# A two-block transformer layer on one core: 512-column products in the gate-and-up stage `gu2`, norms summed by halves after `out2` and `wo2`, and the bias rows copied before the second weight slab

## The chip, the core and the metric

The kernel runs on one core of a Trainium2 chip, as one launch. The metric is the device time of that launch in microseconds, the median of several runs. A profiled execution gives, beside its own time, one record per instruction: start, duration and what released it. Matrix products run on TensorE (PE), elementwise work on VectorE (DVE) and ScalarE (ACT); GpSimd (POOL) and SyncE (SP) here issue DMAs.

## The reference, cut to what matters

The whole computation is one hybrid layer (three attentions, a gated merge, a convolved feed-forward) and then a second block on the same 256 tokens of width 1024. The change touches mostly the second block, and a small table of the first:

```python
def second_block(x, mem, ...):
    mem_n = rms_norm(mem, mem_norm_g)
    h = rms_norm(x, g[0])                      # in2: convolution and RWKV mixing
    ...
    y = jnp.concatenate([y_conv, y_rwkv], axis=-1) @ w_out[i]      # stage out2
    x = x + rms_norm(y, g[1])                                      # norm y1
    y = memory_cross_attention(rms_norm(x, g[2]), mem_n, wq[i], wkv[i], wo[i])   # g2, wq, wo2
    x = x + rms_norm(y, g[3])                                      # norm y3
    y = swiglu(rms_norm(x, g[4]), w_gu[i], w_down[i])              # g4, gu2, down2
    x = x + rms_norm(y, g[5])                                      # norm y5
```

`rms_norm(y, g)` divides each row by the root of its mean square (plus 1e-6) and multiplies by a gain. `swiglu` multiplies by `w_gu` (1024 x 5632), takes silu of the first half times the second, and multiplies by `w_down` (2816 x 1024). In the first block the relative-position bias is a table of 12 heads spread over distances and added to attention scores.

## The kernel before, in words

All products are in fp32 precision made of three: each operand is split into a high part, rounded to the fast type, and the rest, and high x high, high x low and low x high are summed in PSUM (function `three`). The weights come as 126 slabs of 128 x 2048 floats (1 MB). For each slab SP starts the DMA into one of four buffers `raw` when the slab that lay there is used (`slab_used`), ACT makes `w_hi` (`split`, L481), DVE makes `w_lo` (`split`, L1003), and PE waits for `lo_ready`. ACT and DVE run one slab ahead. Each engine has one program in order, written out by hand, and semaphores tie them.

**Feature stages** (`up`, `gu2`, `wq` and others, function `features`) have the weights stationary, 128 columns at a time, and the 256 tokens moving: for each slab two column tiles `c`, in each eight depths `k`, in each three products of 256 columns, 48 in all. A slab's result is a "unit"; unit `u` lies in PSUM bank `u % 2` and must be taken out (`out_freed`) before PE starts unit `u + 2`. **Token stages** (`out2`, `wo2`, `down2`, function `token_products`) have the tokens stationary and 512 weight columns moving; token tile 0 ends in banks 4 and 5, tile 1 in 6 and 7, each bank with half of the 1024 columns. The first two slabs of `up` and `gu2` are computed token-wise by `first_pair`/`token_half`, tile 0 before tile 1, so that PE can start while tile 1 is still being normed.

**`gu2`** has 22 slabs in 11 pairs: even units are gates, odd units values. For pair `p`, ACT takes silu of the gate from PSUM (L958), DVE multiplies it with the value from PSUM (L1691), ACT copies the product's high part to `gT_hi` (L971), DVE subtracts for `gT_lo` (L1285). Pair 0 comes out turned and is transposed by PE into bank 6 (`turn_gu2`) in the middle of slab 3.

**A norm of a product** (`y1` after `out2`, `y3` after `wo2`) runs so for each token tile: ACT squares all 1024 columns from PSUM with a running sum (L498), then takes the root (L503); DVE multiplies PSUM by the gain (L1619), inverts the root (L1033), and scales and adds to `x` (L1625). Then comes the next norm of `x` itself: ACT squares `x` and takes the root, DVE writes `xn` (L1050), PE transposes it (L1780), ACT and DVE split the transposed tile into `hT_hi` (L521) and `hT_lo` (L1057). The last norm, `y5` tile 1, is already done by halves of 512 columns in `before`: PE finishes the first half of the columns first, ACT squares it while PE does the second half, DVE turns that sum into a bias for the root.

**The bias rows**: at the start PE spreads the bias table into PSUM (L1947, L1948), ACT copies the rows out (L563, L564) after its split of slab 2, POOL writes them to DRAM (L426) and reads them back as a sliding 1.5 MB plus 0.75 MB pattern (L432), and DVE adds them to the scores of group 0 (L1129).

## Time and profile before

| | |
|---|---|
| median of three runs | 871.76 us |
| lowest and highest | 871.37 and 872.42 us |
| profiled execution, its own time | 872.74 us |
| its span, first to last instruction | 870.9 us |
| PE busy | 852.4 us (98%) |
| DVE busy | 566.8 us (65%) |
| ACT busy | 445.0 us (51%) |
| granted TensorE clock | 0.998 |

A busy time adds up instructions, a span runs from the first to the last. Matmuls overlap by a modelled tail, so what one product costs in a stream is the distance from its start to the next one's, not its own duration. "Idle before" is the time in which an engine had nothing running before an instruction, with what released it.

### The profile page before, as it was taken

What the parts mean: (1) busy time and instruction counts of PE and PEld (TensorE: products, weight loads), DVE (VectorE), ACT (ScalarE), POOL (GpSimd) and SP (SyncE); (2) the same over time, 40 slices, a digit from 0 to 9 for tenths busy, and PEclk for the clock granted to TensorE, in tenths of its full rate; (3) what the DMA queues carried; (4) which work ended last, traced back from release to release, by engine and by line L of the source; (5) the groups of instructions that cost most, each with busy time, mean ns of one, the idle gap of its engine ahead of it and who ended that gap; (6) DMA issues with size and microseconds to landing.
All of it is one profiled execution on the core that took longest, in us unless ns stands there. A gap on an engine that the chain in (4) does not pass through costs nothing.

```text
span 870.9 us, 18537 instructions
## 1 busy us (share of the span) xinstructions
PE 852.4 (98%) x7972; PEld 790.7 (91%) x7972; DVE 566.8 (65%) x674; ACT 445.0 (51%) x571; POOL 20.8 (2%) x31
## 2 busy tenths in 40 slices
PE   8999999999999999999999999999999999999997
PEld 6989999989999998889997899988987999999885
DVE  6486565575977877638799974667554655545443
ACT  6546855454855566536574311546555544443432
POOL 1110000000000002000000000000000000000000
PEclk9999999999999999999999999999999999999999
DMA  8644454565655555455641211245424455555551
GB/s 333 245 166 146 152 178 154 181 217 199 236 168 182 188 193 186 158 187 177 217 169 71 99 50 53 99 148 194 167 97 150 167 191 193 170 175 186 193 193 49
DMA packets 22114, 145.40 MB, mean 167 GB/s; under 512 B 2603, under 2 KB 2795, under 8 KB 5922
## 3 DMA queue, kind: packets, MB, share of 16 engines
q1 hardware_dynamic: 19008, 134.23, 44.2%
q0 software_dynamic: 2896, 10.13, 3.4%
q8 instruction: 54, 0.88, 0.4%
q14 instruction: 10, 0.08, 0.0%
q10 hardware_dynamic: 146, 0.07, 0.0%
HBM read 143.35 MB, written 1.07 MB: 166 GB/s over the span
## 4 chain that ended last, share of the span: by engine, by line
PE 78%; DVE 10%; DMA 5%; ACT 4%; issue 2%; SPq 0%; POOL 0%; DVEq 0%; ACTq 0%
PE ps L1739 22%; PE ps L1741 21%; PE ps L1740 21%; DMA raw<-in_weights 3%; PE ps L1865 3%; DVE cacc L1383 3%; PE ps L2231 2%; DVE w_lo L1003 2%; DMA bias<-bias_scratch 2%; ACT w_hi L481 1%; PE ps L2426 1%; PE ps L2442 1%; PE ps L2014 1%; PE ps L1805 1%; ACT sc L591 1%
## 5 line engine op out<-in xcount | busy, mean ns | idle before, releaser
L1003 DVE TENSOR_TENSOR w_lo<-raw,w_hi 128x2048 fp32r<-128x2048 f32 x125 | 287.3, 2302 | 126.7 <-ACT w_hi L481 126.5
L1739 PE MATMUL ps<-hT_hi,w_hi 128*128 128x256 f32 x1128 | 321.8, 285 | 0.9 <-ACT sig L636 0.5
L1740 PE MATMUL ps<-hT_lo,w_hi 128*128 128x256 f32 x1128 | 319.1, 283 | 0.0
L1741 PE MATMUL ps<-hT_hi,w_lo 128*128 128x256 f32 x1128 | 319.1, 283 | 0.0
L481 ACT ACTIVATE w_hi<-raw 128x2048 fp32r<-128x2048 f32 x125 | 238.8, 1913 | 138.3 <-DMA raw<-in_weights 138.3
L1739 PEld LDWEIGHTS ps<-hT_hi,w_hi 128*128 128x128 f32 x1128 | 216.3, 192 | 5.5 <-issue 3.6
L1740 PEld LDWEIGHTS ps<-hT_lo,w_hi 128*128 128x128 f32 x1128 | 216.4, 192 | 0.1
L1741 PEld LDWEIGHTS ps<-hT_hi,w_lo 128*128 128x128 f32 x1128 | 216.4, 192 | 0.0
L1741 PE MATMUL ps<-w_hi,gT_lo 128*128 128x512 f32 x176 | 69.3, 394 | 0.0
L1740 PE MATMUL ps<-w_lo,gT_hi 128*128 128x512 f32 x176 | 68.8, 391 | 0.0
L1739 PE MATMUL ps<-w_hi,gT_hi 128*128 128x512 f32 x176 | 68.7, 390 | 0.0
L1302 DVE SCALAR_TENSOR_TENSOR ub<-ps,pvec,ub 128x255 f32<-128x255 f32 (+1 forms) x88 | 38.4, 477 | 25.1 <-ACT ub L676 22.0
L1739 PE MATMUL ps<-w_hi,hT_hi 128*128 128x512 f32 (+2 forms) x128 | 47.0, 368 | 0.0
L1740 PE MATMUL ps<-w_lo,hT_hi 128*128 128x512 f32 (+2 forms) x128 | 46.3, 362 | 0.0
L1741 PE MATMUL ps<-w_hi,hT_lo 128*128 128x512 f32 (+2 forms) x128 | 46.3, 362 | 0.0
L676 ACT ACTIVATE ub<-ps,pvec 128x256 f32<-128x256 f32 x44 | 22.4, 561 | 44.7 <-PE ps L1741 44.7
L1740 PEld LDWEIGHTS ps<-w_lo,gT_hi 128*128 128x128 f32 x176 | 33.0, 188 | 7.5
L1739 PEld LDWEIGHTS ps<-w_hi,gT_hi 128*128 128x128 f32 x176 | 33.1, 188 | 7.1
L1741 PEld LDWEIGHTS ps<-w_hi,gT_lo 128*128 128x128 f32 x176 | 33.1, 188 | 6.9
L1285 DVE TENSOR_TENSOR gT_lo<-ub,gT_hi 128x512 f32 (+1 forms) x21 | 14.5, 688 | 32.4 <-ACT gT_hi L971 31.7
L958 ACT ACTIVATE ub<-ps 128x512 f32<-128x512 f32 x11 | 6.6, 597 | 43.2 <-PE ps L1741 43.1
L1739 PEld LDWEIGHTS ps<-w_hi,hT_hi 128*128 128x128 f32 x128 | 24.1, 189 | 4.5 <-issue 0.7
(325 smaller groups left out, 1187.6 us busy)
## 6 DMA issues: line engine op xcount, KB each, us to landing
raw<-in_weights SPq DMA_DIRECT2D x126, 1024.0 KB, 4.9
row_gain<-in_rows_vec POOLq DMA_DIRECT2D x4, 512.0 KB, 3.9
norm_gain<-in_rows_vec POOLq DMA_DIRECT2D x4, 512.0 KB, 5.5
bias<-bias_scratch POOLq DMA_DIRECT2D x1, 1536.0 KB, 12.7
x<-in_x SPq DMA_DIRECT2D x2, 512.0 KB, 3.9
xn<-in_mem POOLq DMA_DIRECT2D x2, 512.0 KB, 5.9
out<-x SPq DMA_DIRECT2D x4, 256.0 KB, 2.1
masks<-in_masks POOLq DMA_DIRECT2D x1, 768.0 KB, 11.0
```

The costliest lines, as they stand in the source:

```text
L481: A(w_hi[:, n % RAW, :], raw[:, n % RAW, :], ACT.Copy).then_inc(sems["hi_ready"], 1)
L591: A(sc[:, g % 2, i, s:e], sc[:, g % 2, i, s:e], ACT.Exp, bias=ast[:, 88 + col:89 + col], accum_out=ast[:, 120 + col:121 + col]).then_inc(s ...
L676: A(ub[:, p % 2, s, c, :], src[:, c * T:(c + 1) * T], ACT.Identity, bias=pvec[:, bass.ds(p + 2 * turn, 1), col + 3], scale=pvec[:, bass.ds ...
L1003: V.tensor_tensor(w_lo[:, n % RAW, :], raw[:, n % RAW, :], w_hi[:, n % RAW, :].bitcast(F32), ALU.subtract).then_inc(sems["lo_ready"], 1)
L1285: V.tensor_tensor(gT_lo[:, bass.ds(2 * p + 4 * turn, 2), :], src, gT_hi[:, bass.ds(2 * p + 4 * turn, 2), :].bitcast(F32), ALU.subtract)\
L1302: ins = V.scalar_tensor_tensor(out=dst, in0=src[:, c * T:(c + 1) * T - lag], scalar=pvec[:, bass.ds(p + 2 * turn, 1), 4 * (2 * s + c) + ta ...
L1383: ins = V.scalar_tensor_tensor(out=dst, in0=src, scalar=vec[:, col:col + 1], in1=dst, op0=ALU.mult, op1=ALU.add)
L1739: mm(dst, left[0], right[0], start=first, stop=False)
L1740: mm(dst, left[0], right[1], start=False, stop=False)
L1741: return mm(dst, left[1], right[0], start=False, stop=last)
L1865: last = mm(dst, part[:, k, cols], right[:, k * T:(k + 1) * T], start=(part is hT_hi and k == 0 and right is hi), stop=(part is hT_lo and ...
L2231: last = mm(ps[to, b + q, j * CHUNK:(j + 1) * CHUNK], left[rows, 8 * q + j, :], right(rows, 8 * q + j), start=True, stop=True)
```

## The change

**1. `gu2` with 512-column products.** `hT_hi` and `hT_lo` become the two halves of one tile `hT`. From slab 2 of `gu2` on, the new function `doubled` replaces `features`: for each column tile and depth it multiplies the high weights by high and low tokens side by side (512 moving columns, one bank) and adds the low weights times the high tokens on the second half (256 columns). A unit now takes two banks, 0 and 1 or 2 and 3, and its two halves must be added: DVE does it with a `tensor_reduce` over the pair (`gu_sum`), for the gate and for the value. ACT takes silu in place in SBUF, DVE multiplies in SBUF. `doubled` waits for bank 1 before its second column tile in the first doubled slab, as unit 81 (value of pair 0) lies there.

**2. Half-column sums.** `sumsq_halves` (ACT) and `add_halves` (DVE) are the code of `y5` tile 1 as functions, now used for both tiles of `y1` and `y3` also; the product stages before them (`out2`, `wo2`) finish the last slab by halves for both token tiles. After `y1`, the norm `g2` is written in two halves per tile, and ACT fills `hT_hi` before its next split and before the last memory unit is taken out.

**3. The head of `gu2`.** DVE's subtraction for slab 1 is cut in two: one half before the norm of tile 0, the other behind it, with a signal `lo_rest` for the second. `first_pair` runs high rows of both slabs, then low rows of both, and transposes tile 1 only after these.

**4. Bias rows.** ACT copies them before its split of slab 2.

```diff
@@ ACT, the start
-            splits(2)
             act.wait_ge(sems["bias_ps_ready"], 1)
             A(bias_row[0:4, 0, :], ps[0:4, 6, 0:BIAS_ROW], ACT.Copy).then_inc(sems["bias_row_ready"], 1)
             A(bias_row[0:8, 1, :], ps[0:8, 7, 0:BIAS_ROW], ACT.Copy).then_inc(sems["bias_row_ready"], 1)
+            splits(2)
@@ ACT, norms and gu2
+            def sumsq_halves(name, stage, t, halves_ready):
+
+                act.wait_ge(sems["acc_half"], halves_ready)
+                A(tok[:, 0, 0, :], bank(4 + 2 * t), ACT.Square, accum_out=stat[:, 40:41]).then_inc(sems["half_sum"], 1)
+                acc_tile(stage)(t)
+                col = 4 * STATS[name] + t
+                A(tok[:, 0, 1, :], bank(5 + 2 * t), ACT.Square, accum_out=stat[:, col:col + 1]).then_inc(sems["sumsq_ready"], 1)
+                act.wait_ge(sems["half_bias"], halves_ready)
+                act.wait_ge(sems["sumsq_ready"], STAT_AT[name, t])
+                A(stat[:, col + TT:col + TT + 1], stat[:, col:col + 1], ACT.Sqrt, scale=1.0 / D, bias=stat[:, 41:42])\
+                    .then_inc(sems["rms_ready"], 1)
...
-            sumsq("y1", lambda t: banks(4 + 2 * t, 2), acc_tile("out2"))
+            for t in range(TT):
+                sumsq_halves("y1", "out2", t, 1 + t)
...
             sumsq("g2", lambda t: x[:, t, :], x_tile("y1"))
+            fill_normed("g2")
             splits(FIRST_SLAB["wq"])
             memory_out(7)
-            fill_normed("g2")
...
-            sumsq_acc("y3", "wo2", 0)
+            sumsq_halves("y3", "wo2", 0, 3)
             splits(FIRST_SLAB["gu2"])
             sumsq_tile("g4", "y3", 0)
-            sumsq_acc("y3", "wo2", 1)
+            sumsq_halves("y3", "wo2", 1, 4)
             fill_tile("g4", 0)
...
+                if p == 0:
+                    A(gate, unit(u, turn), ACT.Silu).then_inc(out_freed[u % 2], 1)
+                else:
                     gu_high(p - 1, turn)
+                    if p >= 2:
+                        act.wait_ge(sems["g_lo_ready"], PAIRS + p - 1 + 2 * turn)
+                    act.wait_ge(out_freed[u % 2], u // 2 + 1 + 2 * turn)
+                    A(gate, gate, ACT.Silu).then_inc(sems["gate_silu"], 1)
                 split(n + 2 + AHEAD, turn)
@@ DVE, norms
+            def half_bias(halves_ready):
+
+                dve.wait_ge(sems["half_sum"], halves_ready)
+                V.tensor_scalar(stat[:, 41:42], stat[:, 40:41], 1.0 / D, EPS, ALU.mult, ALU.add).then_inc(sems["half_bias"], 1)
...
-            add_normed("y1", 1)
-            normed("g2")
+            for t in range(TT):
+                add_halves("y1", 1, t, 1 + t, 1)
+            normed("g2", (0,), 2)
+            normed("g2", (1,), 2)
...
-            add_normed("y3", 2, tiles=(0,))
-            splits(FIRST_SLAB["gu2"])
+
+            add_halves("y3", 2, 0, 3, 1)
+            n = next_slab[0]
+            next_slab[0] += 1
+            dve.wait_ge(sems["hi_ready"], n + 1)
+            V.tensor_tensor(w_lo[:, n % RAW, 0:SLAB // 2], raw[:, n % RAW, 0:SLAB // 2],
+                            w_hi[:, n % RAW, 0:SLAB // 2].bitcast(F32), ALU.subtract).then_inc(sems["lo_ready"], 1)
             normed("g4", (0,), 2)
-            add_normed("y3", 2, lambda: fill_tile("g4", 0), tiles=(1,))
+            V.tensor_tensor(w_lo[:, n % RAW, SLAB // 2:], raw[:, n % RAW, SLAB // 2:],
+                            w_hi[:, n % RAW, SLAB // 2:].bitcast(F32), ALU.subtract).then_inc(sems["lo_rest"], 1)
+            add_halves("y3", 2, 1, 4, 1)
+            fill_tile("g4", 0)
             normed("g4", (1,), 2)
             fill_tile("g4", 1)
@@ DVE, gu2
+            def gu_sum(p, s, u, turn):
+
+                dve.wait_ge(sems["slab_used"], UNIT_SIGNAL[u][1] + 4 * turn)
+                both = ps[:, 2 * (u % 2):2 * (u % 2) + 2, :]
+                evacuated(u, V.tensor_reduce(ub[:, p % 2, s, :, :], both.rearrange("p c (h n) -> p c n h", h=2), AX.X, ALU.add))
...
+                    gu_sum(p, 0, u, turn)
                 split(n + 2 + AHEAD, turn)
...
+                    dve.wait_ge(sems["gate_silu"], p + 2 * turn)
+                    gu_sum(p, 1, u + 1, turn)
+                    wait_unit(u + 1, turn)
+                    V.tensor_tensor(value, gate, value, ALU.mult).then_inc(sems["gated_value"], 1)
@@ PE
+            def doubled(n, u, turn=0, between=None):
+
+                bank_free(u, turn)
+                hi, lo = slab(n, turn)
+                for c in range(2):
+                    if c and between:
+                        between()
+                    if c and u == FIRST_UNIT["gu2"] + 2:
+                        pe.wait_ge(out_freed[(u - 1) % 2], (u - 1) // 2 + 1)
+                    dst = bank(2 * (u % 2) + c)
+                    for k in range(KD):
+                        w = slice(k * T + c * P, k * T + (c + 1) * P)
+                        mm(dst, hi[:, w], hT[:, :, k, :], start=(k == 0), stop=False)
+                        last = mm(dst[:, T:2 * T], lo[:, w], hT_hi[:, k, :], start=False, stop=(k == KD - 1))
+                return last
...
+                if stage == "gu2":
+                    for low_rows in (False, True):
+                        for s in range(2):
+                            token_half(stage, name, s, 0, low_rows)
+                    transposes(name, 1)
```

PE, one depth after another in slab 2 of `gu2`, before (`w_hi` and `w_lo` are the weight parts, `hT_hi` and `hT_lo` the token parts):

```order
L1739 MATMUL ps<-hT_hi,w_hi 128x256
L1740 MATMUL ps<-hT_lo,w_hi 128x256
L1741 MATMUL ps<-hT_hi,w_lo 128x256
L1739 MATMUL ps<-hT_hi,w_hi 128x256
L1740 MATMUL ps<-hT_lo,w_hi 128x256
L1741 MATMUL ps<-hT_hi,w_lo 128x256
```

and the same place now:

```order
L1805 MATMUL ps<-hT,w_hi 128x512
L1806 MATMUL ps<-hT,w_lo 128x256
L1805 MATMUL ps<-hT,w_hi 128x512
L1806 MATMUL ps<-hT,w_lo 128x256
```

Three products of 256 columns became one of 512 and one of 256; the columns streamed are the same 768.

DVE between the end of `wo2` and the second pair of `gu2`, before (`xn`, `x` the normed and the running tokens, `ub` the gate and value buffers):

```order
L1619 TENSOR_TENSOR xn<-ps,row_gain 128x1024
L1033 RECIPROCAL stat<-stat 128x1
L1625 SCALAR_TENSOR_TENSOR x<-xn,stat,x 128x1024
L1003 TENSOR_TENSOR w_lo<-raw,w_hi 128x2048
L1033 RECIPROCAL stat<-stat 128x1
L1050 SCALAR_TENSOR_TENSOR xn<-x,stat,norm_gain 128x512 x2
L1619 TENSOR_TENSOR xn<-ps,row_gain 128x1024
L1057 TENSOR_TENSOR hT_lo<-ps,hT_hi 128x4x128 x2
```

and now:

```order
L1634 TENSOR_SCALAR stat<-stat 128x1
L1644 TENSOR_TENSOR xn<-ps,row_gain 128x512 x2
L1036 RECIPROCAL stat<-stat 128x1
L1648 SCALAR_TENSOR_TENSOR x<-xn,stat,x 128x1024
L1706 TENSOR_TENSOR w_lo<-raw,w_hi 128x1024
L1036 RECIPROCAL stat<-stat 128x1
L1053 SCALAR_TENSOR_TENSOR xn<-x,stat,norm_gain 128x512 x2
L1709 TENSOR_TENSOR w_lo<-raw,w_hi 128x1024
L1634 TENSOR_SCALAR stat<-stat 128x1
L1644 TENSOR_TENSOR xn<-ps,row_gain 128x512 x2
```

The second `TENSOR_SCALAR` (the bias for the root of tile 1) stands behind the second half of the split, and `hT_lo` of tile 0 has moved behind the whole of tile 1's norm.

DVE in `gu2`, second pair, before:

```order
L1003 TENSOR_TENSOR w_lo<-raw,w_hi 128x2048
L1285 TENSOR_TENSOR gT_lo<-ps,gT_hi 128x512
L1003 TENSOR_TENSOR w_lo<-raw,w_hi 128x2048
L1691 TENSOR_TENSOR ub<-ub,ps 128x512
```

and now:

```order
L1006 TENSOR_TENSOR w_lo<-raw,w_hi 128x2048
L1288 TENSOR_TENSOR gT_lo<-ps,gT_hi 128x512
L1720 TENSOR_REDUCE ub<-ps 128x512
L1006 TENSOR_TENSOR w_lo<-raw,w_hi 128x2048
L1720 TENSOR_REDUCE ub<-ps 128x512
L1738 TENSOR_TENSOR ub<-ub 128x512
```

Two reductions per pair are new; the gate's stands between the low part of the product before and the second split.

## Rows read from the trace of the kernel before

**Rows 1.** The page's first part: busy time and share by engine.

```profile
PE 852.4 (98%) x7972; PEld 790.7 (91%) x7972; DVE 566.8 (65%) x674; ACT 445.0 (51%) x571; POOL 20.8 (2%) x31
```

**Rows 2.** The waits of PE: who, for whom, us in total, times, longest.

```profile
PE ps L1780 <- DVE xn L1050: 3.5, 4, 1.6
PE ps L2001 <- DVE ast L1187: 1.2, 1, 1.2
PE ps L1805 <- ACT hT_hi L521: 1.2, 1, 1.2
```

**Rows 3.** Timeline (start us, duration, engine, line), ACT: silu of two gates in succession.

```profile
718.80 0.60 ACT L958 ACTIVATE ub<-ps 128x512 f32<-128x512 f32 x1 [4.73 <-PE ps L1741]
...
730.31 0.60 ACT L958 ACTIVATE ub<-ps 128x512 f32<-128x512 f32 x1 [4.54 <-PE ps L1741]
```

**Rows 4.** Timeline, PE: 512-column streams in `out2` (first two) and `down2` (last two).

```profile
597.29 0.39 PE L1741 MATMUL ps<-w_hi,hT_lo 128*128 128x512 f32 x1
...
602.05 0.39 PE L1741 MATMUL ps<-w_hi,hT_lo 128*128 128x512 f32 x1
...
856.41 0.39 PE L1739 MATMUL ps<-w_hi,gT_hi 128*128 128x512 f32 x1
...
864.65 0.39 PE L1739 MATMUL ps<-w_hi,gT_hi 128*128 128x512 f32 x1
```

**Rows 5.** Timeline, DVE: a reduction over 1024 elements, and a scan over 256.

```profile
43.25 1.21 DVE L1139 TENSOR_REDUCE ast<-sc 128x4 f32<-128x1024 f32 x1
...
45.03 0.68 DVE L1181 TENSOR_TENSOR_SCAN sig<-masks,sig 4x256 f32<-4x256 f32 x1
```

**Rows 6.** The page's fifth part: costliest groups (busy, mean ns | idle before, releaser).

```profile
L1003 DVE TENSOR_TENSOR w_lo<-raw,w_hi 128x2048 fp32r<-128x2048 f32 x125 | 287.3, 2302 | 126.7 <-ACT w_hi L481 126.5
...
L481 ACT ACTIVATE w_hi<-raw 128x2048 fp32r<-128x2048 f32 x125 | 238.8, 1913 | 138.3 <-DMA raw<-in_weights 138.3
...
L1285 DVE TENSOR_TENSOR gT_lo<-ub,gT_hi 128x512 f32 (+1 forms) x21 | 14.5, 688 | 32.4 <-ACT gT_hi L971 31.7
```

**Rows 7.** Timeline, y3 tile 0 (whole) and y5 tile 1 (second half): square, then add.

```profile
667.59 1.03 ACT L498 ACTIVATE tok<-ps 128x1024 f32<-128x1024 f32 x1 [3.30 <-PE ps L1741]
...
670.14 1.29 DVE L1625 SCALAR_TENSOR_TENSOR x<-xn,stat,x 128x1024 f32<-128x1024 f32 x1
...
865.54 0.60 ACT L987 ACTIVATE tok<-ps 128x512 f32<-128x512 f32 x1 [0.69 <-PE ps L1741]
...
867.06 1.41 DVE L1713 SCALAR_TENSOR_TENSOR x<-xn,stat,x 128x512 f32<-128x512 f32 x2
```

**Rows 8.** Timeline, head of `gu2`: transposes on PE, fills on ACT, the value product on DVE.

```profile
674.54 1.32 PE L1780 MATMUL ps<-masks,xn 128*128 128x128 f32 x8 [1.55 <-DVE xn L1050]
...
681.42 1.32 PE L1780 MATMUL ps<-masks,xn 128*128 128x128 f32 x8 [0.35 <-DVE xn L1050]
...
675.30 1.26 ACT L521 ACTIVATE hT_hi<-ps 128x512 fp32r<-128x512 f32 x2 [0.82 <-PE ps L1780]
...
682.17 1.26 ACT L521 ACTIVATE hT_hi<-ps 128x512 fp32r<-128x512 f32 x2 [1.79 <-PE ps L1780]
...
691.24 0.68 DVE L1691 TENSOR_TENSOR ub<-ub,ps 128x512 f32<-128x512 f32 x1
```

**Rows 9.** Timeline, DVE between `out2` and `wq`: the low fills.

```profile
610.62 2.49 DVE L1057 TENSOR_TENSOR hT_lo<-ps,hT_hi 128x512 fp32r<-128x512 f32 x4 [1.30 <-ACT hT_hi L521]
```

**Rows 10.** Timeline, the start: bias copies, slab splits and exponentials on ACT, bias sum on DVE, DMA on SP.

```profile
21.35 0.46 ACT L563 ACTIVATE sig<-ps 4x384 f32<-4x384 f32 x1
...
30.40 1.91 ACT L481 ACTIVATE w_hi<-raw 128x2048 fp32r<-128x2048 f32 x1
...
39.60 1.91 ACT L481 ACTIVATE w_hi<-raw 128x2048 fp32r<-128x2048 f32 x1 [1.86 <-DMA raw<-in_weights]
...
44.70 0.40 ACT L591 ACTIVATE sc<-sc,ast 128x128 f32<-128x128 f32 x1 [1.41 <-DVE ast L1150]
...
40.79 1.82 DVE L1129 TENSOR_TENSOR sc<-ps,bias 128x768 f32<-128x768 f32 x2 [5.13 <-DMA bias<-bias_scratch]
...
30.04 0.33 SPq L390 DMA_DIRECT2D raw<-in_weights  x1
```

More of the change, by code:

```diff
@@ L1820, in first_slab, with token_products @@
                 first_features(FIRST_SLAB[stage], FIRST_UNIT[stage], ready)
-            def token_products(name, left, ready, then=None, together=1, halves=False):
+            def token_products(name, left, ready, then=None, together=1, halves=()):
                 n0, count = FIRST_SLAB[name], dict(STAGE_SLABS)[name]
@@ L1828, in product @@
                     hi, lo = slab(n0 + i)
-                    by_half = halves and t == 1 and i == count - 1
+                    by_half = t in halves and i == count - 1
                     for one, other in itertools.product(range(2), range(2)):
```

118 lines of the change are left out of this document (60 added, 58 removed).

## The prediction

> **What bounds the kernel now.** I read the page's busy times first, then PE's waits, then the timelines where the change acts. PE is busy 852.4 us of 870.9 [rows 1], so only two things can shorten the kernel much: a cheaper stream of products, or the 18.5 us in which PE has none. Of those the waits name the ones that this change can reach: four waits for `xn`, 3.5 us, of which 1.55 and 0.35 stand at the head of `gu2`; 1.2 us for the first fill of `wq`; 1.2 us for DVE in the first attention group [rows 2, 8]. DVE and ACT have room on average (65% and 51%) [rows 1], but DVE gets new work in `gu2`, so its order there must be followed too.
>
> **1. Products of 512 columns.** Two silus lie 11.51 us apart with 96 products between them, so a 256-column product costs 119.9 ns in a stream [rows 3]. In `out2`, 21 products of 512 columns take 4.76 us, 226.7 ns each; in `down2`, 36 take 8.24 us, 228.9 ns [rows 4]. The difference 226.7 - 119.9 = 106.8 ns is what 256 more columns cost at 2.4 GHz, so about 13.2 ns is fixed per product. Per depth: before 3 x 119.9 = 359.7 ns, after 226.7 + 119.9 = 346.6 ns, 13.1 ns less. A slab has 16 depths: 0.21 us less, 5.55 instead of 5.76 us. For 20 slabs 4.2 us; by the `down2` interval 10.9 ns a depth, 3.5 us. Not shown is a moving operand that lies in two pieces, as `hT[:, :, k, :]` does. From below it costs nothing, as the pieces are 256 floats each; from above I take the whole fixed part a second time, 13.2 ns, which eats the gain. I take nothing: within a piece the reads are those of every row here.
>
> Here a rule of the Trainium skill speaks against the size. TensorE: Matmul & The Clock Gate, section "Back-to-back issue gap", gives a warm interval of N/2.4 + 2.5 ns; by its fixed part 320 fewer products would save 0.8 us, not 4.2. The trace disagrees at 13.2 ns, though it can't say whether that part goes with the product or with the kind of stream.
>
> **2. Does DVE keep up?** Per pair DVE gets two reductions over 1024 PSUM elements. A reduction over 1024 elements takes 1.21 us from SBUF [rows 5]; I take 1.2. Per element the slowest DVE row is the scan, 0.68 us for 256 [rows 5]; at that rate one would take 2.7 us, the upper end. The loop that must fit into a pair, 2 x 5.55 = 11.1 us, runs from one gate sum to the next: ACT silu until its next start 0.5, ACT split 1.94, DVE split 2.21, value sum 1.2, multiplication 0.6, DVE split 2.21, low part 0.6, gate sum 1.2 [rows 5, 6] (on one engine the next start comes about 0.1 us before the end that a duration says). That is 10.5 us, with register work some 10.7: it fits, with 0.4 us to spare. So from slab 3 on `gu2` stays with PE: 19 x 0.21 = **4.0 us** saved. What hides 2.4 us of new DVE work per pair is DVE's idleness before; the wait for the gate sum on ACT has a 1.9 us split queued behind it, which is in the loop above.
>
> **3. Between `wo2` and slab 3 of `gu2`.** For y3 tile 0 the add starts 2.55 us after the square of 1024 columns; in the halved form of y5, 1.52 us after the second square [rows 7]. So the add of tile 0 starts at 669.1 instead of 670.14. Then only half a split (1.2 us) stands before the norm instead of 2.3 [rows 6], and `xn` is there at 672.9; PE ends `wo2` at 674.54 - 1.55 = 673.0, so this wait [rows 8] goes. But a new wait appears. ACT must take the root of y3 tile 1 before it fills `hT_hi` of tile 0, and that root waits for the half bias, which DVE gives only after both halves of `xn` (673.5) and the second half of the split (674.7). The fill starts at 675.0, against 675.30 [rows 8]. Of 1.55 us only 0.3 to 0.4 us is left.
>
> After that PE has 48 products before the transposes of tile 1 instead of 40, so these start at 681.4 as before (681.42), and `xn` is there. Their fill starts at 682.1, against 682.17 [rows 8]. Low rows no longer stand between transposes and high rows, so PE starts tile 1 at 682.7 and slab 2 at 688.5, 0.8 us sooner than before. Now what is late next: the second column tile of slab 2 needs bank 1, free when DVE has multiplied the value of pair 0. It did so 691.24 + 0.68 - 682.17 = 9.75 us after the fill [rows 8], through ACT's split, table load, silu, split and DVE's split, which the change leaves alone: 691.85. PE would want it at 688.5 + 8 x 0.347 = 691.3, and waits 0.6 us. Slab 3 starts at 694.65 instead of 695.05: **0.4 us** gained, slab 2's 0.21 included. If nothing stalled it would be 1.0; if the half bias is later by a fill, 0.
>
> In slab 3 the turned pair passes ACT 0.6, DVE 0.6 and the gate sum 1.2: bank 0 is free 2.45 us after the transposes, PE needs it after 2.77. Value sum 1 ends about 0.05 us late for slab 5. I count 0.
>
> **4. y1 to `wq`.** PE is covered by the last memory slab while the norm runs, so the earlier root buys little; DVE is serial here, and gets two more half instructions per norm, some 0.6 us until the last `xn`. But ACT fills at once instead of after a split and a copy. DVE's fills waited 1.30 us for that [rows 9], the fill that PE waits for among them. 1.30 - 0.55: **0.75 us**; between 0 (DVE slower than I count) and 1.3. ACT's split for `wq` slab 1 moves behind the fills; DVE could not take it before its own fills anyway (610.62 + 2.49 [rows 9]), and PE needs it only a slab, 5.76 us, later.
>
> **5. Bias rows.** ACT can copy at 18.2 instead of 21.35 [rows 10]; it was idle until the slab came, so slab 2 loses nothing. POOL's chain starts 3.1 us sooner. DVE's first bias sum waited 5.13 us for that DMA, and exponentials waited 1.41 us for DVE [rows 10]; with both gone the ACT split at 39.60, the copy and the table load set the exponentials at 43.3, 1.4 us sooner, enough for all of PE's 1.2 us [rows 2]. The danger is the transfer: the slab split at 30.40 [rows 10] now shares the DMA with the bias for longer. ACT then has the forget gate, whose end must be before 39.6; this allows the slab to land up to 32.3. I take **1.2 us**; at worst -0.3, if that slab needs the 9.5 us that the next one took beside the bias, from 30.04 to 39.60 [rows 10].
>
> **Sum.** 4.0 + 0.4 + 0.75 + 1.2 = 6.35 us. Profiled time 872.74 - 6.35 = 866.4; the median of the runs lies 0.98 below the profiled one, so 871.76 - 6.35 = **865.4 us**. The tail (`y5`) only becomes a function and costs nothing.
>
> **Rivals.** A: the fixed part doesn't go, because the split operand or the kind of stream brings it back (also what the page's 2.5 ns comes to): section 1 then gives 0 to 0.8 us and the rest 2.2 (without slab 2's share): 868.7 to 869.6. For it: no row has such an operand. Against: rows 4 give the same fixed part for both widths.
> B, faster: the 256-column product behind one of 512 is cheaper, its weights being loaded meanwhile. If it ran at 113 ns, 7 ns x 304 = 2.1 us more, and bank 1 without the 0.6: 862.7.
> C, slower than before: the reduction over two innermost elements in different places of PSUM runs at the scan's rate. With 2.3 us each the loop is 10.7 + 2.2 = 12.9 us, 1.8 above a pair, over 9 pairs 16 us: 865.4 + 16 = 881. It costs from where the sum passes 1.4 us, and ends slower than before from 10.7 + 2(r - 1.2) = 11.1 + 6.35/9, r = 1.75 us. Against it: DVE rows go by elements, not by place. Between 1.4 and 1.75 lies 866 to 871.5.
> D: the change does nothing at the start, as the slab lands late: 866.6 to 866.9. It is inside the forecast's range.
>
> **How the numbers follow.** Forecast with D, 864 to 868: 0.70. A: 0.12. B: 0.06. C above 1.75: 0.05, between 1.4 and 1.75: 0.07. To hold eight in ten the range takes the forecast, A's first half and B's nearer part: 863.5 to 868.9. A measurement tells 0.2%, 1.7 us, from no change: faster is under 870.0. A lies under that, half of C's middle too: faster 0.90, same 0.04, slower 0.06.
>
> **What would show it.** Silus 11.1 us apart and no PE wait in slabs 3 to 21: step 1 and 2 right. Reductions at 1.2 us in the groups. One PE wait of about 0.6 us in the middle of slab 2, released by DVE's value product. The first fill of `g4` about 0.3 us sooner, with ACT's root released by DVE's half bias. No PE wait near 49 us. PE's waits at `wq` 0.75 us less. Wrong would be: a silu distance of 11.5 (A), DVE without idle time in `gu2` (C), or ACT waiting for the slab at 30 us past 32.3 (D).

## The result and the profile after

The changed kernel takes 867.60 us (median of 6 runs, 866.89 to 869.08), the kernel before 872.52 us beside it (6 runs, 871.37 to 873.13). The ratio is 0.9947, with a 95% interval of 0.9933 to 0.9960: 4.6 us less, between 3.5 and 5.8. The forecast was 6.35 us less (865.4 us, range 863.5 to 868.9). The direction and the range held. The sum was 1.7 us too large, and not all of its terms were right.

The profiled execution took 867.52 us (before 872.74), its span is 865.6 us (before 870.9). First the page's busy line and two groups of its fifth part (busy us, mean ns | idle before), in answer to [rows 1, 6]:

```profile
PE 849.6 (98%) x7652; PEld 774.0 (89%) x7652; DVE 589.1 (68%) x705; ACT 447.4 (52%) x579; POOL 20.9 (2%) x31
...
L1006 DVE TENSOR_TENSOR w_lo<-raw,w_hi 128x2048 fp32r<-128x2048 f32 x124 | 284.8, 2300 | 136.6 <-ACT w_hi L481 136.3
...
L1805 PE MATMUL ps<-hT,w_hi 128*128 128x512 f32 x320 | 111.7, 393 | 0.0
```

320 products are gone, and DVE has 22.3 us more to do. The new group on DVE, from the groups by line, is the reduction, at the 1.2 us that the forecast took from [rows 5]:

```profile
L1720 DVE TENSOR_REDUCE ub<-ps 128x512 f32<-128x1024 f32 x20 | 24.4, 1218 | 0.7 <-PE ps L1806 0.7
```

PE's waits after (who, for whom, us in total, times, longest), in answer to [rows 2]:

```profile
PE ps L1918 <- ACT hT L521: 2.2, 3, 1.4
PE ps L1831 <- DVE xn L1053: 1.3, 1, 1.3
...
PE ps L2064 <- DVE ast L1190: 0.6, 1, 0.6
...
PE ps L1856 <- ACT hT L521: 0.3, 1, 0.3
PE ps L1856 <- DVE hT L1060: 0.2, 1, 0.2
```

The wait for `xn` is one instead of four (L1831; the one left is at the first norm). L1856 is `wq`: 0.5 us instead of 1.4. L1918 is the head of `gu2`: there the wait for `xn` became one for ACT's fill. L2064, the first attention group, went from 1.2 to 0.6.

Now the stream of `gu2` itself. The timeline of PE (start us, duration, engine, line) at the first product of slab 7, of slab 21 and of `down2`, which follows it:

```profile
716.33 0.39 PE L1805 MATMUL ps<-hT,w_hi 128*128 128x512 f32 x1
...
793.99 0.39 PE L1805 MATMUL ps<-hT,w_hi 128*128 128x512 f32 x1
...
799.53 0.39 PE L1774 MATMUL ps<-w_hi,gT_hi 128*128 128x512 f32 x1
```

and the same two places before (there the slab has 48 products):

```profile
718.51 0.28 PE L1739 MATMUL ps<-hT_hi,w_hi 128*128 128x256 f32 x1
...
799.15 0.28 PE L1739 MATMUL ps<-hT_hi,w_hi 128*128 128x256 f32 x1
```

14 slabs take 77.66 us instead of 80.64; by 14 x 16 depths that is 346.7 ns a depth (one product of 512 columns and one of 256) instead of 360.0 (three of 256). The forecast had 346.6. It reads like a full confirmation of step 1. It isn't, as the experiments show.

### The profile page after: what moved, and what is told of

It is laid out like the page before. It is cut to its first block, busy times and chain, and to the rows that moved or that the text cites. A ratio compares the mean times of both kernels' runs of the same rounds, so it can differ in the third digit from the quotient of the medians.

```text
span 865.6 us, 17964 instructions
## 1 busy us (share of the span) xinstructions
PE 849.6 (98%) x7652; PEld 774.0 (89%) x7652; DVE 589.1 (68%) x705; ACT 447.4 (52%) x579; POOL 20.9 (2%) x31
## 4 chain that ended last, share of the span: by engine, by line
PE 87%; ACT 4%; DMA 4%; DVE 3%; issue 1%; POOL 0%; ACTq 0%; DVEq 0%; SPq 0%
PE ps L1774 19%; PE ps L1775 18%; PE ps L1776 18%; PE ps L1805 9%; PE ps L1806 4%; PE ps L1918 4%; PE ps L2300 2%; DMA bias<-bias_scratch 2%; ACT w_hi L481 1%; PE ps L2263 1%; DMA raw<-in_weights 1%; PE ps L1831 1%; PE ps L2495 1%; PE ps L2511 1%; PE ps L2005 1%
## 5 line engine op out<-in xcount | busy, mean ns | idle before, releaser
L1774 PE MATMUL ps<-hT,w_hi 128*128 128x256 f32 x808 | 231.0, 286 | 0.5 <-ACT sig L636 0.4
L1775 PE MATMUL ps<-hT,w_hi 128*128 128x256 f32 x808 | 228.5, 283 | 0.0
L1776 PE MATMUL ps<-hT,w_lo 128*128 128x256 f32 x808 | 228.5, 283 | 0.0
L1774 PEld LDWEIGHTS ps<-hT,w_hi 128*128 128x128 f32 x808 | 154.9, 192 | 4.8 <-issue 3.6
L1775 PEld LDWEIGHTS ps<-hT,w_hi 128*128 128x128 f32 x808 | 155.0, 192 | 0.1
L1776 PEld LDWEIGHTS ps<-hT,w_lo 128*128 128x128 f32 x808 | 154.9, 192 | 0.0
L1805 PE MATMUL ps<-hT,w_hi 128*128 128x512 f32 x320 | 111.7, 393 | 0.0
L1806 PE MATMUL ps<-hT,w_lo 128*128 128x256 f32 x320 | 89.6, 280 | 0.0
L1805 PEld LDWEIGHTS ps<-hT,w_hi 128*128 128x128 f32 x320 | 59.9, 187 | 13.9 <-DVE ub L1733 0.3
L1806 PEld LDWEIGHTS ps<-hT,w_lo 128*128 128x128 f32 x320 | 60.5, 189 | 0.0
L1774 PE MATMUL ps<-w_hi,hT 128*128 128x512 f32 (+2 forms) x128 | 47.0, 368 | 0.0
L1775 PE MATMUL ps<-w_lo,hT 128*128 128x512 f32 (+2 forms) x128 | 46.3, 362 | 0.0
L1776 PE MATMUL ps<-w_hi,hT 128*128 128x512 f32 (+2 forms) x128 | 46.3, 362 | 0.0
## 6 DMA issues: line engine op xcount, KB each, us to landing
bias<-bias_scratch POOLq DMA_DIRECT2D x1, 1536.0 KB, 11.5
```

Of the source, the lines that this page charges most:

```text
L1774: mm(dst, left[0], right[0], start=first, stop=False)
L1775: mm(dst, left[0], right[1], start=False, stop=False)
L1776: return mm(dst, left[1], right[0], start=False, stop=last)
L1805: mm(dst, hi[:, w], hT[:, :, k, :], start=(k == 0), stop=False)
L1806: last = mm(dst[:, T:2 * T], lo[:, w], hT_hi[:, k, :], start=False, stop=(k == KD - 1))
```

## The experiments

The kernel before took 871.8 to 872.6 us beside each group of runs.

**One part at a time.** Four kernels carry one part of the change each, on top of the kernel before. The first moves the two copies only:

```diff
-            splits(2)
             act.wait_ge(sems["bias_ps_ready"], 1)
             A(bias_row[0:4, 0, :], ps[0:4, 6, 0:BIAS_ROW], ACT.Copy).then_inc(sems["bias_row_ready"], 1)
             A(bias_row[0:8, 1, :], ps[0:8, 7, 0:BIAS_ROW], ACT.Copy).then_inc(sems["bias_row_ready"], 1)
+            splits(2)
```

> The kernel before with the two bias-row copies ahead of ACT's split of slab 2, nothing else. Theory (from the trace of the changed kernel): the rows' way to DRAM and back is held up by weight transfers, so the bias comes about when it did and PE's wait for DVE near 50 us stays above 0.6 us; gain 0 to 0.4 us. Rival (the prediction's step 5): the bias comes 3 us sooner, the wait of 1.2 us goes, gain 1.2 us; it would hold if the changed kernel's start was only an unlucky run, its small inputs having landed 1 us late.

Measured: 871.84 us (871.08 to 874.96, 11 runs), ratio 0.9998 (0.9988 to 1.0008). By the ratio the gain is 0.2 us, between -0.7 and 1.0: the move alone gives nothing that can be told from zero, and the 1.2 us of the prediction's step 5 fall. The wait at the first attention group is 0.65 us in this trace, and slab 4 of the weights was not late in it (its split started at 30.98 us).

The second has `doubled` and `gu_sum` alone, with the old norms, first pair and fills:

```diff
-                    used(features(n0 + j, u0 + j, None, between=turned))
+                    if name == "up":
+                        used(features(n0 + j, u0 + j, None, between=turned))
+                    else:
+                        used(doubled(n0 + j, u0 + j, between=turned))
```

> The kernel before with the 512-column products and the half sums of gu2 alone, nothing of the norms, of the head of gu2 or of the start. Theory: a depth costs 346.7 ns from the fifth or sixth doubled slab on, 13.3 ns less than before, and the first doubled slabs lose some 0.9 us of the 4.3 to bank waits, so 3.3 to 3.7 us are gained. Rival: the losses in the first slabs come from the changed head (value product of pair 0 too late for bank 1), which this kernel lacks; then 4.0 to 4.3 us.

Measured: 869.88 us (868.15 to 870.79, 10 runs), ratio 0.9967 (0.9957 to 0.9976): 2.9 us less (2.1 to 3.8), under the numbers of both expectations, though 3.3 lies within the interval. PE at slabs 7 and 21 of its profiled run:

```profile
718.18 0.40 PE L1784 MATMUL ps<-hT,w_hi 128*128 128x512 f32 x1
...
797.33 0.40 PE L1784 MATMUL ps<-hT,w_hi 128*128 128x512 f32 x1
```

79.15 us for the 14 slabs, 353.3 ns a depth: half of the gain is missing, with no wait in between. The profiled run was the longest of the ten (870.79).

The third has the y1 part alone (norm by halves, fills ahead of the split):

```diff
-            sumsq("y1", lambda t: banks(4 + 2 * t, 2), acc_tile("out2"))
+            for t in range(TT):
+                sumsq_halves("y1", "out2", t, 1 + t)
...
+            fill_normed("g2")
             splits(FIRST_SLAB["wq"])
             memory_out(7)
-            fill_normed("g2")
```

> The kernel before with the half-column sums of y1, g2 normed in halves, and ACT filling before its split. Theory: as in the changed kernel, PE reaches the query stage 1.3 us sooner relative to the end of out2, against 0.75 predicted; gain 1.3 us. Rival: 0.75, the rest of the distance in the changed kernel having come from elsewhere.

Measured: 871.07 us (870.11 to 874.54, 11 runs), ratio 0.9989 (0.9980 to 0.9998): 1.0 us less.

The fourth has the way from `wo2` to slab 2 alone (y3 by halves, the split in two halves, the new order in `first_pair`):

```diff
-            sumsq_acc("y3", "wo2", 0)
+            sumsq_halves("y3", "wo2", 0, 1)
...
+                if stage == "gu2":
+                    for low_rows in (False, True):
+                        for s in range(2):
+                            token_half(stage, name, s, 0, low_rows)
+                    transposes(name, 1)
```

> The kernel before with the half-column sums of y3 and the new head of gu2, its slabs from 2 on still with 256-column products. Theory: the fill of g4 tile 0 waits for ACT's root behind DVE's half bias, but PE still starts slab 2 0.5 to 0.8 us sooner, and no bank is waited for, as unit 82 needs bank 0 alone: gain 0.5 to 0.8 us. Rival: the bank of unit 83 (bank 1) is late instead, or nothing remains: 0.

Measured: 871.60 us (870.34 to 873.09, 11 runs), ratio 0.9991 (0.9982 to 1.0000): 0.8 us less. On its trace the way from ACT's last square of `wo2` to the first product of `down2` is 131.40 us against 131.88 before, 0.5 us less. The four add up to 0.2 + 2.9 + 1.0 + 0.8 = 4.9 us, and the whole gave 4.6: within their intervals no part lives on another.

**The y1 part taken apart.** One step of it alone, ACT's fills ahead of its split, with the norms of y1 and g2 in the old form (the last part of the diff of the third kernel).

> The kernel before with one step of the y1 part alone: ACT fills hT_hi for wq before it splits slab 1 of wq and copies, not after. The norm of y1 stays in its old form, without halves. Theory (the 1.30 us that DVE waited for ACT is all that this order cost; the halved norm costs DVE nothing, but brings nothing either): the first product of wq comes 1.1 to 1.3 us sooner after the last product of out2 than before, as in the run with the whole y1 part, and the time is 871.1 to 871.5. Rival (the halved norm gives 0.4 us or more of it, by an earlier root): 0.6 to 0.9 us sooner, 871.8.

Measured: 871.17 us (870.29 to 872.54, 11 runs), ratio 0.9984 (0.9976 to 0.9993). On the trace, time is taken from ACT's square of tile 1, which starts as soon as PE has ended `out2`, to the first product of `wq`. Before 602.48 to 611.64, 9.16 us. Now:

```profile
601.21 1.03 ACT L498 ACTIVATE tok<-ps 128x1024 f32<-128x1024 f32 x1 [1.28 <-PE ps L1741]
...
609.61 0.71 PE L1805 MATMUL ps<-hT_hi,w_hi 128*128 128x256 f32 x4 [0.40 <-ACT hT_hi L521]
```

8.40 us, and the low rows don't wait (0.22 us before), so 0.98 us are gained by the order. In the changed kernel, which has the whole y1 part:

```profile
602.29 0.60 ACT L883 ACTIVATE tok<-ps 128x512 f32<-128x512 f32 x1 [0.60 <-PE ps L1776]
...
610.16 0.71 PE L1856 MATMUL ps<-hT,w_hi 128*128 128x256 f32 x4 [0.27 <-ACT hT L521]
611.09 0.74 PE L1856 MATMUL ps<-hT,w_hi 128*128 128x256 f32 x4 [0.21 <-DVE hT L1060]
...
607.77 1.42 DVE L1053 SCALAR_TENSOR_TENSOR xn<-x,stat,norm_gain 128x512 f32<-128x512 f32 x2
609.15 2.48 DVE L1060 TENSOR_TENSOR hT<-ps,hT 128x512 fp32r<-128x512 f32 x4
```

7.87 us, with the wait for low rows as before: 1.3 us gained. So the order is worth 1.0 and the halves 0.3, between the two expectations; by the time alone the two kernels can't be told apart. It isn't an earlier root that gives the 0.3: the last `xn` ends 6.9 us after that square in the changed kernel, 6.8 before and in this one. What differs is that PE no longer waits for `xn` (0.41 us here) before the transposes of tile 1, as it can begin with the first half of it. DVE's low fills follow `xn` without idle time; they waited 1.30 us before [rows 9].

**The loop through ACT and DVE.** In the changed kernel each reduction of `gu2` is done twice; nothing else is altered:

```diff
+                V.tensor_reduce(xn[:, p % 2, 512 * s:512 * s + 512].rearrange("p (c n) -> p c n", c=2), both.rearrange("p c (h n) -> p c n h", h=2), AX.X, ALU.add)
                 evacuated(u, V.tensor_reduce(ub[:, p % 2, s, :, :], both.rearrange("p c (h n) -> p c n h", h=2), AX.X, ALU.add))
```

> The changed kernel with every reduction of gu2 done twice on DVE (the first into scratch that nothing reads), 20 reductions of 1.2 us more; all else and the result as they are. Theory (the loop through ACT and DVE takes 10.6 us a pair with the reduction at 1.22 us, and PE's two slabs 11.1): 10.6 + 2 x 1.2 = 13.0 us a pair, so silus 13.0 us apart, PE waiting 1.9 us in each of 9 pairs: 17 us more, 884.5 us (883 to 886). Rival (there is slack outside this loop, the splits can run ahead, so that DVE's busy time alone counts: 4 splits' and reductions' sum of about 9.9 us a pair with the doubling stays below 11.1): within 1 us of the changed kernel, 867.6 to 868.6 us.

Measured: 885.83 us (885.26 to 887.34, 4 runs), ratio 1.0149; 18.2 us over the changed kernel's median, a little more than the 17 expected. ACT's silus, first in this kernel and then in the changed one, where they are catching up after the head and so run at the loop's own pace:

```profile
740.42 0.63 ACT L972 ACTIVATE ub<-ub 128x512 f32<-128x512 f32 x1 [4.33 <-DVE ub L1721]
753.27 0.63 ACT L972 ACTIVATE ub<-ub 128x512 f32<-128x512 f32 x1 [4.32 <-DVE ub L1721]
```

```profile
752.22 0.63 ACT L972 ACTIVATE ub<-ub 128x512 f32<-128x512 f32 x1 [3.20 <-DVE ub L1720]
762.82 0.64 ACT L972 ACTIVATE ub<-ub 128x512 f32<-128x512 f32 x1 [3.19 <-DVE ub L1720]
...
784.35 0.63 ACT L972 ACTIVATE ub<-ub 128x512 f32<-128x512 f32 x1 [3.54 <-DVE ub L1720]
795.45 0.63 ACT L972 ACTIVATE ub<-ub 128x512 f32<-128x512 f32 x1 [3.70 <-DVE ub L1720]
```

12.85 us a pair against 10.60, two reductions' starts (1.13 us each) more. From 784.35 on the changed kernel is at PE's pace, 11.10 us a pair. The loop is the one that the forecast drew (10.5 to 10.7 us), and there is no slack outside it: what is added to it beyond 0.5 us a pair, PE pays.

**The head of `gu2`.** In the changed kernel ACT's root for y3 tile 1 waits for DVE's half bias, behind half a split:

```profile
671.96 1.22 DVE L1709 TENSOR_TENSOR w_lo<-raw,w_hi 128x1024 fp32r<-128x1024 f32 x1
673.10 0.15 DVE L1634 TENSOR_SCALAR stat<-stat 128x1 f32<-128x1 f32 x1
...
673.28 0.29 ACT L886 ACTIVATE stat<-stat 128x1 f32<-128x1 f32 x1 [1.07 <-DVE stat L1634]
673.48 1.06 ACT L521 ACTIVATE hT<-ps 128x512 fp32r<-128x512 f32 x2
...
674.20 0.35 PE L1918 MATMUL ps<-w_hi,hT 128*128 128x256 f32 x1 [1.44 <-ACT hT L521]
```

The edit takes that one instruction of 0.15 us from its old place and puts it ahead of the half split:

```diff
-                half_bias(halves_ready)
+                if halves_ready != 4:
+                    half_bias(halves_ready)
...
             normed("g4", (0,), 2)
+            half_bias(4)
             V.tensor_tensor(w_lo[:, n % RAW, SLAB // 2:], raw[:, n % RAW, SLAB // 2:],
```

> The changed kernel with one instruction of DVE moved: the half bias of y3 tile 1 (0.15 us) stands ahead of the second half of the split of slab 1 of gu2 (1.22 us), not behind it. Theory (ACT's root of tile 1, and with it the first fill of g4, wait for that instruction alone): the root starts some 1.0 us sooner, the fill at about 672.5 instead of 673.5, PE's wait of 1.4 us at the first product of gu2 shrinks to 0.4 to 0.6; but bank 1 then is asked for sooner and DVE's value product is not given sooner than ACT's and DVE's queues allow, so 0.5 to 0.9 us of the 1.0 stay: 866.7 to 867.1 us. Rival (what ends the wait is the fill's own chain, xn and the transposes): same time as the changed kernel, 867.6 us.

Its timeline at the same place:

```profile
671.54 0.15 DVE L1634 TENSOR_SCALAR stat<-stat 128x1 f32<-128x1 f32 x1
...
671.89 0.29 ACT L886 ACTIVATE stat<-stat 128x1 f32<-128x1 f32 x1
...
672.81 0.35 PE L1920 MATMUL ps<-w_hi,hT 128*128 128x256 f32 x1 [0.47 <-ACT hT L521]
```

PE's wait is 0.47 instead of 1.44 us, and this is kept until slab 6: counted from ACT's last square of `wo2` (671.11 here, 671.52 in the changed kernel), slab 6 starts 38.27 us later against 39.27. Yet the time is 867.82 us (867.35 to 868.77, 5 runs), no less than the changed kernel's and over the 866.7 to 867.1 expected. Where the 1.0 us went in the profiled run, slabs 7 and 21 tell:

```profile
715.02 0.40 PE L1807 MATMUL ps<-hT,w_hi 128*128 128x512 f32 x1
...
794.17 0.40 PE L1807 MATMUL ps<-hT,w_hi 128*128 128x512 f32 x1
```

79.15 us, the same longer interval as in the kernel with `doubled` alone: 1.49 us lost to 77.66.

In the next kernel DVE also multiplies the value of pair 0 ahead of the split that stood before it (the first added line keeps the split in its place for all other pairs).

```diff
-                split(n + 2 + AHEAD, turn)
+                    split(n + 2 + AHEAD, turn)
...
                     evacuated(u + 1, V.tensor_tensor(value, gate, src, ALU.mult))
+                    split(n + 2 + AHEAD, turn)
```

> As the one before (half bias first), and besides DVE multiplies the value of pair 0 ahead of the split of slab n+3, which frees bank 1 for the second half of slab 2 about 2 us sooner. Theory (the waits inside slab 2 come from bank 1): the gap in the middle of slab 2 goes (0.2 to 0.3 us in the changed kernel, more with the earlier head), so 0.3 us under the one before, unless the split of slab 4 moved behind the product is late for PE, which shows as a wait for DVE at the start of slab 4. 866.2 to 866.8 us. Rival (bank 1 is no bound): the same as the one before, or slower by the late split.

Measured: 867.60 us (865.51 to 869.08, 6 runs), the profiled run 866.60. The pause of 0.2 us in the middle of slab 2 is gone, and slabs 7 and 21 stand at

```profile
715.42 0.39 PE L1808 MATMUL ps<-hT,w_hi 128*128 128x512 f32 x1
...
793.07 0.39 PE L1808 MATMUL ps<-hT,w_hi 128*128 128x512 f32 x1
```

77.65 us, the short interval. Both edits are seen on the timeline; their 1.3 us together (slab 6 starts 38.01 us after that square) are less than what the interval adds or takes, and the medians don't show them.

**The bias rows.** The changed kernel with the two copies put back (the first diff reversed).

> The changed kernel with the copies of the bias rows put back behind the split of slab 2 (step 5 undone). Theory (the bias move is worth next to nothing, as the rows' way through DRAM takes longer when it starts earlier): the time stays within 0.5 us of the changed kernel's, so 867.1 to 868.1 us, and PE's wait at the first attention group is about 1.2 us as before. Rival (the move is worth 1.2 us, and what the single run of it showed was chance): 868.8 us.

Measured: 869.66 us (869.38 to 871.16, 6 runs), 2.1 us over the changed kernel's median. Neither number was right. Its profiled run (870.30 us) is 2.8 us over the changed kernel's. Of these, 1.7 us are the longer interval (slab 7 at 717.50, slab 21 at 796.65, 79.15 us; over slabs 6 to 21 that is 16 x 16 depths of 6.6 ns). The kernel with the half bias first has it too, with the copies in their new place. Another 0.9 us has come together where `out2` ends (603.03 against 602.09), with a wait of 1.2 us at the first attention group instead of 0.6, and a pause of 0.7 us on PE at 46.73 for which the profile shows no releaser (0.25 us in the kernel with `doubled` alone, none in the other traces).

Is that 0.9 us the place of the copies? The fourteen traces, before and after among them, speak against it. Up to the end of `out2` their kernels differ in the copies and little else. In two of them the small inputs came late. Of the other twelve, the five with the copies in the old place ended `out2` at 600.93 to 603.03 us, the seven with the new place at 601.38 to 602.39, and both means are 601.9. The wait at the first attention group is 0.6 to 1.2 us in the six traces with the old place, 0.6 to 1.1 in the eight with the new. So neither the wait nor the start is tied to the move. One trace of each kernel can't say how the 2.1 us between the medians divide, and up to 1.0 us for the move lies within the interval of its own run.

Next, the changed kernel with SyncE waiting for the rows before it asks for slab 4 of the weights:

```diff
             turns = SLABS // RAW - 1
+            sp.wait_ge(sems["bias_rows_out"], 32)
             with sp.Fori(0, turns) as turn:
```

> The changed kernel, but SyncE waits until the bias rows are in DRAM before it asks for slab 4 of the weights, so no slab shares the DMA with them. Theory (the early rows take 3.3 us instead of 1.7 because that slab's transfer is under way): they take 1.7 us again, GpSimd's read of the bias begins at about 22.4 instead of 24.4 us, and DVE's first bias sum starts at 38.5 to 40.5 instead of 41.1. The slab is asked for 4 us later, so ACT's split of it at 33.0 may move to 34 or 35. The time: from 0.5 us less (bias first) to 1.0 us more (slab late), 867.1 to 868.6. Rival (what holds the rows is the write to DRAM itself or the queue, whatever else runs): 3.3 us again, and the time only goes up, 868 to 869.

The start of the changed kernel, GpSimd and DVE:

```profile
20.32 0.52 POOL L426 DMA_DIRECT2D bias_scratch<-sig  x1 [10.47 <-ACT sig L563]
...
24.39 2.10 POOL L432 DMA_DIRECT2D bias<-bias_scratch  x2 [3.05 <-DMA bias_scratch<-sig]
...
41.13 1.82 DVE L1132 TENSOR_TENSOR sc<-ps,bias 128x768 f32<-128x768 f32 x2 [2.83 <-DMA bias<-bias_scratch]
```

and of this one:

```profile
19.32 0.52 POOL L427 DMA_DIRECT2D bias_scratch<-sig  x1 [9.92 <-ACT sig L564]
...
21.78 2.10 POOL L433 DMA_DIRECT2D bias<-bias_scratch  x2 [1.45 <-DMA bias_scratch<-sig]
...
40.69 1.82 DVE L1133 TENSOR_TENSOR sc<-ps,bias 128x768 f32<-128x768 f32 x2 [2.20 <-DMA bias<-bias_scratch]
```

GpSimd waits 1.45 us for the rows instead of 3.05, so a slab in transfer is what holds them. But though the bias is asked for 2.6 us sooner, its sum starts only 0.4 us sooner, a little past the 40.5 expected: from request to landing its two parts took 13.0 and 17.8 us instead of 11.5 and 15.7. PE's wait at the first attention group is 1.1 us. The time is 868.84 us (868.53 to 871.25, 6 runs), with the longer interval in `gu2`. Why the early request gives nothing is in the windows (PE, PEld, DVE, ACT, POOL busy; granted clock, share of the DMA engines, GB/s) of the changed kernel and then of this one:

```profile
28.00:38.00 10.00, 10.00 (x88) 8.68 (x87) 4.83 (x4) 3.79 (x3) 0.00 (x0) 1.00 1.01 361
```

```profile
28.00:38.00 10.00, 10.00 (x89) 8.68 (x88) 5.10 (x4) 4.65 (x4) 0.00 (x0) 1.00 1.00 374
```

For these ten microseconds the DMA engines are full. The bias is 2.3 MB (1536 and 768 KB) and shares them with weight slabs of 1 MB each: by estimate, 2.3 + 2.1 MB for two slabs is 12 us at 361 GB/s. So its end is set mostly by bytes, not by its start. In the twelve traces of fourteen whose small inputs reached PE at 16.7 to 17.8 us the bias sum started between 40.6 and 41.7, wherever the copies stood (in the other two those inputs were later, 18.9 and 19.5, and the sum at 41.7 and 42.7). The Trainium skill, DMA: Bandwidth & Descriptors, section "Specifications", gives about 358 GB/s as a core's limit to HBM. 361 is near that and 374 is 4% over it, so here it is a size to reckon with, not a bound.

**The longer interval.** In the seven traces with this order of products and no doubled reduction a depth takes either 346.7 or 353.3 ns from slab 7 on, and stays there until the end of the stage. Could it be the operand in two pieces, the unknown that step 1 named? In this kernel high and low row of a depth lie side by side:

```diff
-        hT = sb("hT", [P, 2, KD, T], F32R, shared)
-        hT_hi, hT_lo = hT[:, 0, :, :], hT[:, 1, :, :]
+        hT = sb("hT", [P, KD, 2, T], F32R, shared)
+        hT_hi, hT_lo = hT[:, :, 0, :], hT[:, :, 1, :]
```

> The changed kernel with another layout of the operand: hT is 128 x 8 x 2 x 256, the high and low row of a depth side by side, so that the 512 columns of the doubled product are one piece of memory instead of two; the 256-column reads then lie 2 KB apart from depth to depth. Theory P (the second, longer interval of 353 ns a depth comes from the jump between two pieces): 346.5 ns in every slab from 2 to 21, also in 2 to 4; at least 0.3 us less than the profiled changed kernel, 867.2 us or less, and runs closer together, 866.3 to 867.4 us. Rival Q (it comes from how a 512-column and a 256-column product follow each other, whatever the layout, and which of the two intervals runs is decided at a stall): 352 to 354 ns again at least in slabs 2 to 4, and times spread over 866.8 to 869.1 us as for the changed kernel.

Measured: 868.84 us (867.57 to 869.64, 5 runs). Slab 7 starts at 716.83 and slab 21 at 795.98: 79.15 us again, so the jump between two pieces isn't what makes the interval long. Last, the two widths in another order, on top of the version with both edits at the head:

```diff
-                        mm(dst, hi[:, w], hT[:, :, k, :], start=(k == 0), stop=False)
-                        last = mm(dst[:, T:2 * T], lo[:, w], hT_hi[:, k, :], start=False, stop=(k == KD - 1))
+                        if k % 2 == 0:
+                            mm(dst, hi[:, w], hT[:, :, k, :], start=(k == 0), stop=False)
+                            mm(dst[:, T:2 * T], lo[:, w], hT_hi[:, k, :], start=False, stop=False)
+                        else:
+                            mm(dst[:, T:2 * T], lo[:, w], hT_hi[:, k, :], start=False, stop=False)
+                            last = mm(dst, hi[:, w], hT[:, :, k, :], start=False, stop=(k == KD - 1))
```

> The version with the half bias first and the value product first, and one edit more: in every odd depth of a doubled slab the 256-column product comes before the 512-column one, so that equal widths follow each other half of the time. In the runs so far a depth takes either 346.7 or 353.3 ns, and the start-to-start time behind a 512-column product was 230.2 ns in the one and 236.6 in the other, that behind a 256-column product 116.6 ns in both. Theory (the extra 6.5 ns is paid where a 256-column product follows one of 512): there are half as many such places, two depths take 236.6 + 120.0 + 116.6 + 226.8 = 700.0 ns, 350.0 each where the longer interval rules (0.9 us less over 17 slabs), or 346.8 where the shorter one does; 865.5 to 867.5 us. Rival (it belongs to the slab's pattern as a whole and is taken at a stall): 353 ns or 346.7 again, 865.5 to 869.1 us as without the edit. Another order could also cost more: then 355 ns or more and over 868.5 us.

Measured: 866.50 us (865.98 to 867.76, 5 runs), ratio 0.9940 (0.9926 to 0.9954). Slabs 7 and 21:

```profile
714.86 0.40 PE L1809 MATMUL ps<-hT,w_hi 128*128 128x512 f32 x1
...
792.89 0.40 PE L1809 MATMUL ps<-hT,w_hi 128*128 128x512 f32 x1
```

78.03 us, 348.3 ns a depth, a third value, and neither 346.8 nor 350.0: the start-to-start times behind a product don't carry over to another order. So the order of the widths has a part in the interval. It is the lowest median of all kernels here, but its interval overlaps with the changed kernel's, and one trace doesn't show that 348.3 is its only value.

## Why the prediction was right, and where it was not

**Step 1, products of 512 columns.** The profiled run agrees to the nanosecond (346.7 against 346.6), and in that there is luck. Only the sum agrees: the forecast put it together from 226.7 and 119.9 ns, and measured are 230.0 ns behind the product of 512 columns and 116.7 behind that of 256. And of the seven profiled kernels with this order of products and no doubled reduction, only two ran from slab 7 on at 346.7 ns a depth (13.3 less than before), and five at 353.3 (6.7 less). Over 20 slabs this is 4.3 or 2.1 us. The forecast took the short one and had 3.5 us as its lower value, from a stream of equal widths [rows 4]; no row of before has widths in turn, and there the assumption "the fixed part goes with the product" failed. Of 13.3 ns a depth, half comes back in most traces. The rule of the Trainium skill, TensorE: Matmul & The Clock Gate, section "Back-to-back issue gap", would have given, by estimate, 0.8 us by its 2.5 ns. Neither interval agrees with it; the section itself calls that rule the gap of an isolated product. Rival A, that the fixed part comes back, was thus half right in five traces of seven, at a chance of 0.12.

**Step 2, DVE keeps up.** Right: reductions of 1.22 us, the loop 10.60 us, and doubling them moved the pair to 12.85. The silus 11.1 us apart and reductions at 1.2 us are two of the signs that the forecast named. Rival C had its mechanism right (with slower reductions the loop does decide) and the price of a reduction wrong (2.3 us).

**Slabs 3 to 21** gave 3.55 us in the profiled run (PE's starts against before: 1.83 us sooner at slab 3, 5.38 at `down2`), not 4.0. Slabs 3 and 4 ran at the longer interval, and at slab 5 value sum 1 was late, 0.17 us rather than 0.05:

```profile
703.86 1.22 DVE L1720 TENSOR_REDUCE ub<-ps 128x512 f32<-128x1024 f32 x1
...
704.84 0.28 PE L1806 MATMUL ps<-hT,w_lo 128*128 128x256 f32 x1
705.13 0.50 PE L1805 MATMUL ps<-hT,w_hi 128*128 128x512 f32 x1
```

**Step 3, the head.** Right in its mechanism: the root behind the half bias, the wait for bank 1 in slab 2 (0.2 us, not 0.6), 0.33 us from `wo2` to slab 3 where 0.4 stood. The wait named there was a real one: moving one instruction returned 1.0 us of timeline. Alone, the part measured 0.8 us, with an interval of 0 to 1.6.

**Step 4, y1.** Right in kind, too small: 1.3 us on the trace, 1.0 in the run of its own, against 0.75. The failed term is the 0.55 us subtracted for DVE's extra half instructions. They made the last `xn` end 0.06 us later, counted from ACT's last square of `out2` (it started at 607.77 instead of 608.04 and took 1.42 us instead of 1.28). And `xn` in halves gave PE the transposes of tile 1 without a wait, which the step did not count: ACT filled at 608.45 instead of 609.94.

**Step 5, the bias rows.** Wrong: 1.2 us forecast, 0.2 (-0.7 to 1.0) measured alone. The step that failed is "with both gone": it let DVE's wait for the bias go with GpSimd's earlier start. The rows took 3.3 us to DRAM instead of 1.7, and even when they did not (SyncE waiting for them) the bias sum started only 0.4 us sooner, as the DMA was full. The step saw the contention as a danger to the slab only, not as what sets the bias itself. So forecast D, a variant inside the forecast, was the case, by another cause than it gave: the slab was read at 33.03, past 32.3, but the exponentials still waited for DVE (0.58 us), and in the kernel with the copies alone the slab was on time (30.98) and the gain was missing all the same.

Point by point the sum becomes 3.55 + 0.33 + 1.3 + 0 = 5.2 us, the difference of the two profiled runs (872.74 - 867.52). (Two small terms nearly cancel: `out2` ended 0.2 us sooner, and the changed kernel's own time is 0.15 us more above its span.) The medians differ by 4.9 us, and the ratio says 4.6; that runs with the longer interval are among them would explain it, but was not seen.

## What to carry to other kernels

A fixed cost per instruction that is read from a stream of one shape need not hold where shapes alternate; take the nearest mixed stream, or keep half of it as the lower bound. When a DMA is started earlier, first ask for the share of the DMA engines between its start and its landing: if that is near 1, as here, an earlier start gives little, and what would have to change is the bytes that share this stretch. And where an engine's small result is waited for by another (here 0.15 us of DVE), put it ahead of any long instruction that nobody waits for.

## What was not expected of the hardware

One and the same stream of 512- and 256-column products ran at 346.7 or 353.3 ns a depth, with no wait in either, and both at a granted clock of 1.0, the 2.4 GHz level. And one execution can take both. The timeline of the kernel with the half bias first has, in slab 4 and from slab 5 on:

```profile
698.86 0.39 PE L1807 MATMUL ps<-hT,w_hi 128*128 128x512 f32 x1
...
703.02 0.39 PE L1807 MATMUL ps<-hT,w_hi 128*128 128x512 f32 x1
...
703.63 0.50 PE L1807 MATMUL ps<-hT,w_hi 128*128 128x512 f32 x1
...
705.13 0.40 PE L1807 MATMUL ps<-hT,w_hi 128*128 128x512 f32 x1
705.37 0.28 PE L1808 MATMUL ps<-hT,w_lo 128*128 128x256 f32 x1
705.49 0.40 PE L1807 MATMUL ps<-hT,w_hi 128*128 128x512 f32 x1
```

From 698.86 to 703.02 lie 12 depths, 346.7 ns each. Then comes the pause before slab 5 (0.61 us from start to start), and from 705.13 to slab 7 (715.02) lie 28 depths of 353.2 ns. In the longer interval 236.7 ns pass on the mean behind the 512-column product, in the changed kernel's shorter one 230.0, and behind the other 116.7 in both.

All seven traces began at the longer one in slab 2. The changes mostly stand behind a pause, and they go both ways. In the changed kernel and in the one with the value product first, the short interval came in behind the pause at slab 5. In two others (half bias first, old place of the copies) it came in behind the pause in slab 2, and went again behind the transposes in slab 3. In the five kernels with the longer interval from slab 7 on, the pause at slab 5 was followed by it. Once the short one came in with no pause to be seen (in slab 4 of the kernel above). So what picks the interval is open: the layout does not, the order of the widths has a part in it, and a pause can turn it either way. How often each comes from run to run was not seen, as there is one trace of each kernel; the spread of the runs (3.6 us for the kernel with the value product first, 1.8 us for the one with swapped pairs) is no more than a hint.
